# First group and a half of the output projection, and part of the residual's loads, moved into the gated attention's last tiles; the gated attention's opening in another order

## What is computed

```python
o_g, s_new = gla_chunked(q_g, k_g, v_g, log_a, gla_s0)       # 4 heads, key 64, value 128
o_g = rms_norm(o_g, g_gla_out).reshape(B, T, GLA_V_WIDTH) * jax.nn.silu(r_g)
x = x + ga1 * (jnp.concatenate([o_sb, o_g], axis=-1) @ w_out)
h2 = rms_norm(x, g_ffn) * (1.0 + sc2) + sh2
x = x + ga2 * (jnp.square(jax.nn.relu(h2 @ w_up)) @ w_down)
```

## Time and profile before

| what | value |
|---|---|
| time, median of 3 runs (lowest to highest) | 1725.63 us (1725.63 to 1729.12) |
| the profiled execution's own time | 1724.33 us |
| its span in the profile | 1722.5 us |
| PE busy | 1615.6 us (94%) |
| DVE, ACT, POOL busy | 861.0, 641.1, 588.9 us |
| granted TensorE clock, mean of the span | 0.965 |
| gated stage in the span | 714.1 to about 834 us |
| output stage begins | 834.4 us |

### The profile page before, as it was taken

The page is one execution under the profiler, slowest core; times in us unless marked ns, Lnnn a source line. Parts: engine busy times, 40 slices in busy tenths (PEclk is TensorE's granted clock), DMA queues, the critical chain, the costliest instruction groups (busy, mean ns, idle before and its releaser), DMA issues. The chain is left out here.

```text
span 1722.5 us, 27695 instructions
## 1 busy us (share of the span) xinstructions
PE 1615.6 (94%) x11224; PEld 1409.2 (82%) x11224; DVE 861.0 (50%) x1299; ACT 641.1 (37%) x995; POOL 588.9 (34%) x316
## 2 busy tenths in 40 slices
PE   5899999999979999898699899999999999999997
PEld 3898998777755455566599799999999999999997
DVE  2501031444547787779314722332223677676776
ACT  3512120332328888566335422111122233232233
POOL 0121212222211000101245444455544566767670
PEclk9899999999989999888799999999999999999999
DMA  9222226676446000264633133344334644333222
GB/s 346 65 102 88 77 85 216 202 218 207 131 176 203 1 25 1 62 206 156 205 100 112 59 118 121 112 140 140 124 125 141 234 154 152 132 137 126 87 103 104
DMA packets 145492, 227.88 MB, mean 132 GB/s; under 512 B 9146, under 2 KB 82317, under 8 KB 144854
## 3 DMA queue, kind: packets, MB, share of 16 engines
q1 hardware_dynamic: 140144, 209.31, 36.1%
q0 software_dynamic: 5120, 16.78, 3.1%
q10 hardware_dynamic: 102, 0.03, 0.0%
HBM read 173.39 MB, written 52.71 MB: 131 GB/s over the span
## 5 line engine op out<-in xcount | busy, mean ns | idle before, releaser
L3092 DVE TENSOR_TENSOR mlp_a<-mlp_relu 128x384 f32<-128x384 f32 (+1 forms) x96 | 104.0, 1087 | 254.7 <-ACT mlp_relu L2959 254.1
L502 PE MATMUL psum<-op_hi,out_first_hi 128*128 128x384 f32 (+1 forms) x528 | 177.6, 336 | 9.9 <-PEq L1817 8.4
L504 PE MATMUL psum<-op_hi,out_first_lo 128*128 128x384 f32 (+1 forms) x528 | 173.6, 329 | 0.0
L2894 POOL TENSOR_TENSOR mlp_a_sums<-mlp_a 128x544 f32<-128x544 f32 x75 | 106.5, 1452 | 173.2 <-DVE mlp_a L3092 169.8
L502 PE MATMUL psum<-op_hi,out_hi 128*128 128x384 f32 (+1 forms) x480 | 159.7, 333 | 0.0
L503 PE MATMUL psum<-op_lo,out_first_hi 128*128 128x384 f32 (+1 forms) x480 | 158.2, 330 | 0.0
L2959 ACT ACTIVATE mlp_relu<-psum 128x384 f32<-128x384 f32 (+1 forms) x96 | 45.4, 473 | 298.9 <-PE psum L504 298.8
L504 PE MATMUL psum<-op_hi,out_lo 128*128 128x384 f32 (+1 forms) x480 | 156.5, 326 | 0.0
L503 PE MATMUL psum<-op_lo,out_hi 128*128 128x384 f32 (+1 forms) x480 | 156.4, 326 | 0.0
L3040 DVE SCALAR_TENSOR_TENSOR x1T<-psum,modT,x1T 128x272 f32<-128x272 f32 (+1 forms) x256 | 115.3, 478 | 70.6 <-PE psum L3123 70.6
L502 PEld LDWEIGHTS psum<-op_hi,out_first_hi 128*128 128x128 f32 x528 | 100.6, 191 | 13.0 <-issue 11.0
(11 more groups left out here) (398 smaller groups left out, 4556.4 us busy)
## 6 DMA issues: line engine op xcount, KB each, us to landing
mlp_t_raw<-mlp_aT SPq DMA_DIRECT2D x21, 1088.0 KB, 5.5
mlp_aT<-mlp_a_sums SPq DMA_DIRECT2D x75, 272.0 KB, 2.0
sa_k<-in_cache_k SPq DMA_DIRECT2D x64, 256.0 KB, 3.0
sa_v<-in_cache_v POOLq DMA_DIRECT2D x64, 256.0 KB, 3.8
out_raw<-in_w_up SPq DMA_DIRECT2D x16, 1024.0 KB, 5.9
out_raw<-in_w_out SPq DMA_DIRECT2D x12, 1024.0 KB, 4.9
mlp_quad_even<-in_w_down SPq DMA_DIRECT2D x9, 1024.0 KB, 8.0
in_raw<-in_w_in SPq DMA_DIRECT2D x8, 1024.0 KB, 6.5
```

The source lines that it names most:

```text
L502: pe.matmul(out, w_hi, x_hi, start=(k == 0), stop=False)
L504: return pe.matmul(out, w_lo, x_hi, start=False, stop=(k == nk - 1))
L2894: pool.tensor_tensor(ts[:, nth % NTS], quadrant(aq[p % 2], k0, t0), quadrant(aq[p % 2], k1, t1), ALU.add if sign > 0 else ALU.subtract).th ...
L3092: dve.tensor_tensor(aq[p % 2][:, m, t0:t0 + tw], r[i % 3][:, 0:tw], r[i % 3][:, 0:tw], ALU.mult).then_inc(s_sq, 1)
```

## The change

**At the end of the gated stage.** `split_lo` moves from iteration 8 to the end of iteration 7, and no longer waits for the last `output`. PE, after its last `sample_outer`, makes slices 0 to 3 of group 0, then `turn_out(8)`, then slices 4 to 7 of group 0 and slices 0 to 3 of group 1; they need only tiles 0 to 2 of the prompt. The last `fin_lo` goes from POOL to DVE. SP issues, behind the first panel, the loads of x tiles 0 to 4 (when DVE has made the queries of tile 8) and of panel 1 (when the last scores are masked), into places of the next stage that are free by then.

**In the output stage.** SP has left x tiles 6, 7, 5, the samples' x, and panel 2 onwards. DVE makes the rest of panel 1 instead of POOL. PE begins with three `turn`s, then slices 4 to 7 of group 1, and goes on from group 2 as before. ACT's first copies wait only for the prompt's stores.

**At the opening of the gated stage.** PE takes the scores of tile 0 between conditioning chunks 0 and 1, and cuts chunk 1 in two. ACT copies the rows of chunk 1 ahead of the first gate, where the copy stood behind the norms of tile 0. DVE makes `key_distances(0)` before it needs queries and keys, and `masked_queries` behind the keys of tile 0.

The diff, its core:

```diff
-OUT_HI_AT, OUT_LO_AT = 143104, 159488
+OUT_RAW1_AT, OUT_HI_AT, OUT_LO_AT, OUT_X_AT = 134912, 143104, 159488, 180224
+X_BUFFER = [2, 3, 4, 5, 6, 7, 0, 1, 8]
+X_AHEAD = 5
...
+        self.offsets = OUT_RAW1_AT, OUT_HI_AT, OUT_LO_AT
+        self.raw1 = g.named(shaped(g.at("out_second_raw", P, KD * PANEL, F32, OUT_RAW1_AT)), "out_second_raw")
+        self.x = [g.at(f"out_x_ahead{t}", P, D, F32, OUT_X_AT + 4 * D * X_BUFFER[t]) for t in range(X_AHEAD)]
...
+    def load_x(self, sp):
+        for t in range(X_AHEAD):
+            sp.dma_start(self.x[t], self.g.io["x_prompt"][0][t * P:(t + 1) * P]).then_inc(self.s_x[t], 16)
+
+    def load_second(self, sp):
+        sp.dma_start(self.raw1, self.g.io["w_out"][0][:, PANEL:2 * PANEL].rearrange("(k p) c -> p k c", p=P)).then_inc(self.s_second, 16)
+
+    def products(self, pe, j, ks):
+
+        t0, tw = CHUNKS[0]
+        cols = slice(j * P, (j + 1) * P)
+        for k in ks:
+            last = three_products(pe, self.g.bank[j + 1][:, 0:tw], self.hi[:, k, cols], self.lo[:, k, cols],
+                                  self.g.op_hi[:, k, t0:t0 + tw], self.g.op_lo[:, k, t0:t0 + tw], k, KD)
+        if ks[-1] == KD - 1:
+            last.then_inc(self.s_mm, 1)
...
                 sp.wait_ge(s_am, 4 * NADA)
                 sp.dma_start(first[:], io["w_out"][0][:, 0:PANEL].rearrange("(k p) c -> p k c", p=P)).then_inc(first_out.s_loaded, 16)
+                sp.wait_ge(s_qd, 3 * NT)
+                first_out.load_x(sp)
+                sp.wait_ge(s_pt, N9)
+                first_out.load_second(sp)
                 sp.wait_ge(s_st, 4 * NT)
...
-                        sp.dma_start(outp[h, m], st[HALF[h], 2 * m + h, :]).then_inc(s_out, 16)
...
-                        sp.dma_start(outs[h, m], s0[HALF[h], :, 2 * m + h, :]).then_inc(s_out, 16)
...
-                for n in range(N9):
+                for n in range(N9 - 1):
                     fin_lo(n)
...
@@ -1987,11 +2017,13 @@
                 ada_rows(0)
                 copy_kn(0)
                 for n in range(N9):
+                    if n == 0:
+                        ada_rows(1)
                     gate_ln(n)
                     if n == 0:
                         rest_exps()
                     norms(n)
-                    if n + 1 < NADA:
+                    if 0 < n < NADA - 1:
                         ada_rows(n + 1)
...
+                def key_distances(i):
...
+                key_distances(0)
                 dve.wait_ge(gated.s_q, 16)
                 dve.wait_ge(gated.s_k, 16)
...
-
-                def key_distances(i):
...
+                    if i == 0:
+                        dve.wait_ge(s_c, 11)
                     mask = (tri[:] if i else tri8).rearrange("k (o t) -> k o t", o=1).to_broadcast([rows, GH, rows])
...
-                key_distances(0)
-                masked_queries()
                 scores(0)
...
                     if n < NT:
                         keys(n)
+                    if n == 0:
+                        masked_queries()
                     if n + 1 < NT:
                         key_distances(n + 1)
...
-                    if n == NT:
-                        dve.wait_ge(s_kt, N9)
-                        dve.wait_ge(s_oo, N9)
-                        first_out.split_lo(dve)
                     if n + 1 < N9:
                         scores(n + 1)
+                    if n == NT - 1:
+                        dve.wait_ge(s_kt, N9)
+                        first_out.split_lo(dve)
+                dve.wait_ge(s_fh, N9)
+                dve.tensor_tensor(g.op_lo[:, GH:2 * GH, tile(NT - 1)], fin[NT % 2], g.op_hi[:, GH:2 * GH, tile(NT - 1)],
+                                  ALU.subtract).then_inc(s_f8, 1)
...
                 ada(0, range(4))
-                ada(1, range(4))
                 pe.wait_ge(s_d, 9)
                 turn_keys(0)
                 score(0)
+                ada(1, (0, 1))
                 turn_ada(0)
                 turn_keys(1)
+                ada(1, (2, 3))
                 score(1)
                 for n in range(N9):
...
                     if n > 0:
                         sample_outer(n - 1)
+                pe.wait_ge(first_out.s_lo, 1)
+                pe.wait_ge(s_fl, 4)
+                first_out.products(pe, 0, range(0, 4))
                 turn_out(NT)
+                first_out.products(pe, 0, range(4, KD))
+                first_out.products(pe, 1, range(0, 4))
...
+        assert g.offsets["out_x0"] == OUT_X_AT
+        x = first.x + [buffers[X_BUFFER[i]][:] for i in range(X_AHEAD, 9)]
...
-                panel(1)
-                for i in range(8):
-                    if i == 7:
-                        sp.wait_ge(s_states, 8 * 16)
-                    sp.dma_start(x[i][:], xp[i * P:(i + 1) * P]).then_inc(s_x[i], 16)
+                for i in (6, 7, 5):
+                    if i == 5:
+                        sp.wait_ge(s_states[1], 4 * 16)
+                    sp.dma_start(x[i], xp[i * P:(i + 1) * P]).then_inc(s_x[i], 16)
                 sp.dma_start(x[8][0:TS], xs).then_inc(s_x[8], 16)
                 for l in range(2, NL):
                     sp.wait_ge(w.lo_done, l - 1)
...
-                pool.wait_ge(s_states, 8 * 16)
+                pool.wait_ge(s_states[1], 4 * 16)
                 pool.memset(ones[:], 1.0).then_inc(s_c, 1)
-                pool.wait_ge(w.lo_done, 1)
-                lo(1)
+                pool.wait_ge(w.lo_done, 2)
                 for j in range(NG):
...
                 round_hi(1)
-                act.wait_ge(s_states, 8 * 16)
+                act.wait_ge(s_states[0], 4 * 16)
                 for j in range(2):
                     copy_turn(j)
...
+                    if j == 0:
+                        act.wait_ge(s_states[1], 4 * 16)
                     act.activation(sq[j % 2][:, 0:tw], g.x1T[:, k, t0:t0 + tw], ACT.Square).then_inc(s_sq, 1)
...
+                dve.wait_ge(w.hi_done, 2)
+                dve.tensor_tensor(w.lo[1][:], w.raw[1], w.hi[1][:], ALU.subtract).then_inc(w.lo_done, 1)
                 for j, (c, kc) in enumerate(groups):
...
-                    b = g.bank[j % 3]
+                    b = g.bank[(j + 1) % 3]
                     dve.wait_ge(s_mm, j + 1)
                     dve.wait_ge(s_xc, j + 1)
...
-                    for k in range(KD):
-                        cols = slice(m * P, (m + 1) * P)
-                        last = three_products(pe, g.bank[j % 3][:, 0:tw], w.hi[l % 2][:, k, cols], w.lo[l % 2][:, k, cols],
-                                              g.op_hi[:, k, t0:t0 + tw], g.op_lo[:, k, t0:t0 + tw], k, KD)
-                    last.then_inc(s_mm, 1)
                     if j == 0:
                         turn(0)
                         turn(1)
                         pe.wait_ge(s_c, 1)
+                        turn(2)
+                        continue
+                    if j == 1:
+                        first.products(pe, 1, range(4, KD))
+                        turn(3)
+                        sum_squares(0)
+                        continue
+                    for k in range(KD):
+                        cols = slice(m * P, (m + 1) * P)
+                        last = three_products(pe, g.bank[(j + 1) % 3][:, 0:tw], w.hi[l % 2][:, k, cols], w.lo[l % 2][:, k, cols],
+                                              g.op_hi[:, k, t0:t0 + tw], g.op_lo[:, k, t0:t0 + tw], k, KD)
+                    last.then_inc(s_mm, 1)
```

40 lines of the change are left out of this document (23 added, 17 removed).

## The result

| | before | after |
|---|---|---|
| median of the runs on one chip | 1725.91 us (1725.63 to 1729.12, 4 runs) | 1708.75 us (1707.6 to 1710.9, 4 runs) |
| ratio | | 0.9898, 95% interval 0.9881 to 0.9915 |
| profiled execution: time, span | 1724.33, 1722.5 us | 1707.6, 1706.0 us |

The change is faster by 1.0%. That the sum came out so near is luck: the opening and two stretches behind it gave 6.8 us more than their terms, and a wait that the sum put at nothing, with the slow group behind it, took 4.6 back.

The account below looks back on a forecast made before the run. PE, busy for 94% of the span, was taken as the bound, with idle holes at opening, border and residual. Group 4 14.9 us earlier gives 1724.33 - 14.9 = 1709.4, plus 1.3 for the median: 1710.7 us, range 1705.5 to 1718.5.

Parts of the forecast that it names:

- The opening, taken at 4.0: Gated stage's opening: scores 1.3 to 3.0 us earlier, PE's 2.26 wait for ACT's copy gone; 4.0 taken from 1.9 to 6.6.
- the high end: Opening: a denser PE might hold the higher clock level, halving the sample queries; at most 3.0 us more, 6.6 in all.
- Rival 2: Opening yields only its low end, POOL's selects holding up DVE's key and query products; 2.1 us less, 1712.8, chance 0.12.
- the rule's low end: Opening: DVE's products with keys and queries, now beside POOL's selects, are held up by 1.7 us, leaving 1.9.
- 3.5 go back into the split, 1.1 come back: DVE before the border: earlier `split_lo` takes 3.5 us of the opening's gain; a shorter `gate` returns 1.1.
- a shift is passed on: Between opening and border DVE sets the pace, so a shift there is passed on and nothing is won.
- PE to the border: After the last `sample_outer`, 36 products and `turn_out(8)` keep PE until 832.5; the border opens at 833.2, set by PE.
- Rival 1: PE stays at 1.2 GHz to the border, which opens 3.2 us later; gain 11.1 us, 1714.6, chance 0.15.
- From the border to group 2: Start of the output stage: three turns, then 12 products, a turn and a sum; 7.0 us taken, group 2 at 840.2.
- From group 2 to group 4: Output stage: groups 2 and 3 take 10.6 us; panel 2 lands at 842.5, so no wait for the square.
- rival 3: Panel 2 becomes the wait, at group 1's sum of squares in front of group 3; up to 8 us, 1718.7, chance 0.10.
- Rival 4: The holes are covered by something unseen, such as a border waiting for stores; within 3.4 us of before, chance 0.03.

Follow-up runs that it names:

- in the run: Changed kernel with ACT's opening order of before: the copy of chunk 1's conditioning rows behind the norms of tile 0 again; ratio to before 0.9923.
- PE's or DVE's old order: Two kernels, each the changed one with only PE's or only DVE's opening order of before; ratios to before 0.9904 (PE) and 0.9941 (DVE).
- end alone: Changed kernel with the opening's old order on PE, ACT and DVE; 1713.6 us, ratio to before 0.9937.
- opening alone: Kernel before with only the opening's new order on PE, ACT and DVE; 1719.11 us, ratio to before 0.9964.
- x tiles behind: Changed kernel with x tiles 0 to 4 loaded at the start of the output stage, panel 1 and products still ahead; ratio to before 0.9955.
- after again: The changed kernel, unchanged, timed and profiled a second time; 1704.74 us, ratio to before 0.9897.
- panel 2 first: Changed kernel with panel 2 issued as the output stage's first load, ahead of x tiles 6, 7, 5 and sample rows; 1704.13 us, ratio to before 0.9900.

## Why the prediction was right, and where it was not

- **The opening, taken at 4.0, gave 7 to 8** (state product at 32.4 before, 24.3 to 25.5 after). Its terms were right: the scores start 1.9 us earlier, inside the 1.3 to 3.0, and the copy's 2.26 is 1.8 in the run. What failed is the choice "I take 4.0, near the lower end": the level of 2.4 GHz, put at the high end with 3.0 us and sample queries alone, held, and over scores, first output and sample queries together it saved 3.56 + 1.97 + 6.10 - 2.00 - 1.08 - 3.65 = 4.9. These three, 1.9, 2.26 and 4.9, are the 9.1 us by which `turn_ada(1)` comes earlier; the new wait of 2.59 for `gl_pt` takes part of it back. The runs with PE's or DVE's old order show what the level hangs on: with 2.03 us, or 1.66 and 0.85 us, of idle time in front of the scores it is lost, with 0.65 it is kept. The length of the idle time does not decide alone, since 1.88 to 2.33 us in front of a sum of squares cost nothing; what does is open.
- **Rival 2, POOL's selects beside DVE's products**, came only in small: one product took 1.02 us where it took 0.29 before, so 0.7 of the 1.7 us moved with it, and DVE waited 0.66 more for POOL's selects in front of `gl_pt` (719.30, above), a wait that the prediction did not have. The Trainium skill (SBUF — State Buffer, Who interferes with whom) makes the pair of ports that DVE shares with GpSimd an exclusive lock. The row of 1.02 agrees, but the products in front of it kept their lengths beside the first selects, and the rule's low end did not come.
- **What passes to the border.** "3.5 go back into the split, 1.1 come back" is a price of 2.4; the run with the end alone shows 2.4 (109.7 to 112.1), and after shows 8.0 - 2.4 = 5.6 against 5.5 measured, a fit closer than the spread of 2.3 us allows. That it depends on PE's level, and is free in the other course, was not in the prediction. Nor does "a shift is passed on" hold whole: in the opening alone 7.0 us arrived as 3.8.
- **PE to the border** was put at 10.9 us from the last sample_outer, and took 9.55, mostly since `turn_out(8)` between the products took 0.35 us of PE's time (822.26 to 822.61) where 1.1 were counted; PE set the border, as said. Rival 1 (the lower level to the border) fell: PE had left it after 8 or 9 products (a granted clock of 0.50 from 818.9 to 821.3 us, 1.00 from 821.5 to 826.9).
- **From the border to group 2** 7.0 were taken and 5.6 measured: the products behind the third turn ran at the upper level (a granted clock of 1.00 from 830 to 832 us).
- **From group 2 to group 4** 10.6 were taken, without a wait, and 15.2 measured: this is the step that failed on the other side, and rival 3 came true, in small. Panel 2 was to land 9.3 us behind the border, by 416 GB/s from a window of before; it landed 11.5 and 10.3 behind it, at 265 and 303 GB/s in the two windows above, while PE came 1.4 sooner than I had it. The wait of 3.06 and the slow restart (6.81 us from sum to sum against 5.24 in the second profile) were the price. The Trainium skill (DMA: Bandwidth & Descriptors, Bandwidth) gives 341 GB/s for one megabyte, in transfers that GpSimd issues; here SP issues them. By that figure the prediction's estimate was a landing 1.5 us later, which was nearer than mine, and the two windows above lie lower than either rate.
- **The sum**: 14.9 + 4.0 (opening) + 1.35 (border) + 1.4 (group 2) - 4.6 (group 4) + 0.5 (the stage began earlier) = 17.5; group 4 came 17.3 earlier. The gain is of the size forecast because these misses offset each other, and the 0.5 is chance. Rival 4 (holes covered by something unseen) fell. The end's term was thus right for the border and the x tiles, and the wait it uncovered was the rival I had given 0.10.

## What to carry to other kernels

When a stall is taken away, follow the buffer that is late next with the rate and the queue of the new order, not with the old window's: here a megabyte that stood fifth in the queue took back 2 to 5 us, and products put in front of it were worth less than half their length. Look also at which operation waits in front of which in an engine's program: the square that PE waited for did not need the late buffer. Where two engines hand work to each other closely, count what a denser PE wins by its clock level in the rows at either level, and expect it to be lost again at the next place where PE runs ahead of its partner and waits. Compare places counted from a common row, and take two profiles of one kernel before explaining 2 us.

## What the runs showed of the hardware that I had not expected

- One program at one place ran 16 score products in 1.90 us in one execution and in 3.51 us in another; before the slow one PE had been idle for 2.51 us.
- Behind a wait of 3.06, 3.12 or 3.18 us at the sum of squares in front of group 3 (after, end alone, x tiles behind) the next group took 6.8 us from sum to sum; behind 1.88, 2.13 or 2.33 us (after again, PE's and DVE's old opening) it took 5.24 or 5.25, so the level was kept there.
- With the transfer engines fully busy (shares 1.03 and 1.05) the core moved 416 GB/s in the kernel before and 303 in the one after; with panel 2 first it moved 407 in the same window (832 to 837 us, share 1.06). The windows differ in what they carry, x tiles with rows of 4 KB or a panel with rows of 1 KB; whether that makes the difference was not tried.
